# A trunk of two layers on one core: the begin of each SwiGLU layer in a new order, with T4 from B21 - B11 - T3

## What is computed

```python
def rms_norm(x, g):
    xf = x.astype(jnp.float32)
    y = xf * lax.rsqrt(jnp.mean(xf * xf, axis=-1, keepdims=True) + EPS)
    return (y * g.astype(jnp.float32)).astype(x.dtype)

def swiglu_ffn(h, w_gate_up, w_down):
    gu = jnp.einsum('btd,df->btf', h, w_gate_up)
    g, u = gu[..., :D_FF], gu[..., D_FF:]
    return jnp.einsum('btf,fd->btd', jax.nn.silu(g) * u, w_down)

# in trunk, for each layer i:
        h = rms_norm(x, norm_ffn[i])
        x = x + swiglu_ffn(h, ffn_w_gate_up[i], ffn_w_down[i])
```

## Time and profile before

| what | us |
|---|---|
| median of 3 runs | 1784.62 |
| lowest and highest run | 1777.22, 1785.21 |
| the profiled execution | 1782.1 |
| its span, from first to last instruction | 1780.2 |
| PE busy | 1721.0 |
| DVE busy | 1157.1 |
| ACT busy | 747.5 |
| POOL busy | 133.4 |

### The profile page before, as it was taken

The page is one execution under the profiler, slowest core; times in us unless marked ns, Lnnn a source line. Parts: engine busy times, 40 slices in busy tenths (PEclk is TensorE's granted clock), DMA queues, the critical chain, the costliest instruction groups (busy, mean ns, idle before and its releaser), DMA issues.

```text
span 1780.2 us, 21489 instructions
## 1 busy us (share of the span) xinstructions
PE 1721.0 (97%) x7993; PEld 1433.1 (81%) x7993; DVE 1157.1 (65%) x1638; ACT 747.5 (42%) x1145; POOL 133.4 (7%) x108
## 2 busy tenths in 40 slices
PE   7989999999999999999998999889999999999998
PEld 6867888888888888888786888768888888888887
DVE  5586666666656765655778776875665565576744
ACT  5543333333333335444566564443333333343432
POOL 1010000000000003023123212200000000000000
PEclk9799999999999999999999999999999999999999
DMA  5003332332357333334122113032343332393333
GB/s 174 13 12 125 112 119 89 110 104 91 114 197 284 95 101 90 98 101 116 48 54 66 36 42 90 24 125 89 95 126 99 95 118 89 144 341 101 95 97 117
DMA packets 185786, 188.43 MB, mean 106 GB/s; under 512 B 8354, under 2 KB 138452, under 8 KB 185684
## 3 DMA queue, kind: packets, MB, share of 16 engines
q1 hardware_dynamic: 112884, 150.36, 26.0%
q10 hardware_dynamic: 72800, 36.70, 7.2%
HBM read 137.23 MB, written 44.56 MB: 102 GB/s over the span
## 4 chain that ended last, share of the span: by engine, by line
PE 89%; DVE 6%; issue 2%; ACT 2%; DMA 1%; SPq 0%; DVEq 0%; ACTq 0%
PE bank L744 43%; PE bank L769 24%; PE bank L576 16%; PE bank L952 2%; PE bank L589 1%; PE bank L902 1%; PE bank L654 1%; PE bank L875 1%; DVE f_t L1689 1%; DVE ring L1763 1%; PE bank L638 1%; DMA raw<-in_ffn_w_gate_up 0%; DVE raw_max L2185 0%; DMA raw<-act_d 0%; PE bank L791 0%
## 5 line engine op out<-in xcount | busy, mean ns | idle before, releaser
L744 PE MATMUL bank<-h_T,ring 128*128 128x512 f32 x2112 | 505.0, 392 | 16.8 <-DVE ring L1763 10.8
L744 PEld LDWEIGHTS bank<-h_T,ring 128*128 128x128 f32 x2112 | 397.7, 189 | 104.9 <-issue 13.2
L769 PE MATMUL bank<-a,w 128*128 128x512 f32 x1848 | 421.1, 389 | 1.8 <-DVE a L1837 1.8
L769 PEld LDWEIGHTS bank<-a,w 128*128 128x128 f32 x1848 | 346.3, 188 | 74.3 <-issue 2.6
L744 PE MATMUL bank<-h_B,ring 128*128 128x512 f32 x1584 | 381.3, 390 | 6.5 <-DVE ring L1763 6.3
L744 PEld LDWEIGHTS bank<-h_B,ring 128*128 128x128 f32 x1584 | 296.7, 188 | 69.5 <-DVE ring L1763 7.1
L1763 DVE TENSOR_TENSOR ring<-raw,ring 128x512 fp32r<-128x512 f32 (+1 forms) x180 | 146.5, 815 | 48.9 <-ACT ring L1167 48.5
L1167 ACT CAST ring<-raw 128x512 fp32r<-128x512 f32 (+1 forms) x180 | 128.5, 716 | 76.2 <-PE bank L744 54.7
L1833 DVE TENSOR_TENSOR w<-wd_A,w 128x1024 fp32r<-128x1024 f32 x72 | 82.7, 1149 | 101.9 <-ACT w L1238 101.9
L1238 ACT CAST w<-wd_A 128x1024 fp32r<-128x1024 f32 x72 | 70.6, 981 | 178.4 <-PE bank L769 178.4
L576 PE MATMUL bank<-half_hi,aw 128*128 128x512 f32 x320 | 112.6, 405 | 1.9 <-ACT tmp L1443 1.9
(11 more groups left out here) (178 smaller groups left out, 2060.7 us busy)
## 6 DMA issues: line engine op xcount, KB each, us to landing
act_d<-tmp SPq DMA_DIRECT2D x154, 256.0 KB, 3.3
raw<-in_ffn_w_gate_up ACTq DMA_DIRECT2D x70, 512.0 KB, 4.1
raw<-act_d SPq DMA_DIRECT2D x70, 512.0 KB, 3.6
wd_A<-in_ffn_w_down SPq DMA_DIRECT2D x40, 512.0 KB, 8.3
raw<-in_attn_w_qkv SPq DMA_DIRECT2D x24, 512.0 KB, 4.0
raw<-in_ffn_w_gate_up SPq DMA_DIRECT2D x18, 512.0 KB, 4.4
raw<-in_attn_w_o SPq DMA_DIRECT2D x16, 512.0 KB, 4.0
tmp<-tmp SPq DMA_DIRECT2D x80, 64.0 KB, 2.0
```

The lines of the kernel that those rows point to most:

```text
L744: ins = pe.matmul(out[:, :], w, m, start=k in (1, 2, 5) and j == 0 and t == 0, stop=k in (2, 3, 4) and j == 3 and t == 2, skip_group_check ...
L769: ins = pe.matmul(banks[m][:, :], w, h, start=q in (0, 1, 3) and first and t == 0, stop=q in (1, 5, 6) and jj == NBLK - 1 and t == 2, skip ...
```

## The change

Four things are changed, in both layers, and nothing outside the begin of the SwiGLU stage except where the pieces before it are named.

1. **Squares inside the first product.** The two sums of squares on PE stand between the first three (layer 0) or two (layer 1) pieces of product 1 of chunk 0 and its rest; the spread of the scale (`wide`) stands ahead of product 2 of chunk 0 instead of behind it. On ACT the root comes ahead of the copy of product 1, on DVE the reciprocal comes ahead of `swiglu`.
2. **T4 from B21 - B11 - T3.** B21 - B11 is made in place by four new passes (`d_full`): in layer 0 behind the reciprocal, in layer 1 two of them behind a weight split and two behind the reciprocal. `t4_full` subtracts T3 from it and stands beside `t3_lo`. `t2_lo` no longer waits for T4. `h_tp` now counts T3 first and T4 second.
3. **DVE's and ACT's passes.** Chunk 1's first split stands behind the first `b1_full` and `t1_full`; the pair S2, S4 of chunk 0 stands in the middle of T2; `add_c11` of chunks 0 to 2 stands later; `block_sums` of chunk 2 is cut in two parts, of which the first stands ahead of the splits S1 of chunk 2 and A22 of chunk 1; A11 of chunk 3 is split ahead of S3 and A22 of chunk 2. In `pair_sums` the sum for T2 comes ahead of the one for T3. The table `EARLY` follows the new order.
4. **Block products.** Product 3 of chunk 1 comes ahead of product 7 of chunk 0, and product 1 of chunk 3 between products 6 and 3 of chunk 2.

The diff, cut to its core:

```diff
-        EARLY = {0: (1, 3, 5, 5, 2, 2, 4), 1: (6, 10, 11, 12, 13, 7, 14), 2: (8, 15, 16, 16, 17, 9, 18)}
+        EARLY = {0: (1, 3, 9, 9, 2, 2, 4), 1: (5, 10, 11, 12, 13, 6, 15), 2: (7, 14, 16, 16, 18, 8, 19)}
...
             def swiglu(layer):
                 k = 2 * layer + 1
-                gate_up(layer, 0, 1)
+                first = 3 if layer == 0 else 2
+                gate_up(layer, 0, 1, range(first))
                 if layer == 0:
                     sum_square(1, 14, bank[3])
                 else:
                     mean_square(3, 1, bank[3])
                 sum_square(k, 15, bank[3])
+                gate_up(layer, 0, 1, range(first, 4))
+                wide(k, 1, bank[5])
                 gate_up(layer, 0, 2)
-                wide(k, 1, bank[5])
...
                 gate_up(layer, 1, 6)
+                gate_up(layer, 1, 3)
                 gate_up(layer, 0, 7)
-                gate_up(layer, 1, 3)
...
                 for i in range(2, NF):
-                    if i > 2:
+                    if i > 3:
                         gate_up(layer, i, 1)
                     gate_up(layer, i, 5)
                     gate_up(layer, i, 6)
+                    if i == 2:
+                        gate_up(layer, 3, 1)
                     gate_up(layer, i, 3)
...
             def swiglu(layer):
                 k = 2 * layer + 1
+                root(k, 1, bank[3])
                 snap_p1(layer, 0)
-                root(k, 1, bank[3])
                 w_split(layer, 1, G_A11)
+                t1_hi(layer, 0)
                 w_split(layer, 1, G_A12)
...
                 t2_hi(layer, 0)
+                w_split(layer, 0, G_S2, 2)
+                t2_hi(layer, 1)
                 snap_p5(layer, 0)
                 w_split(layer, 1, G_S1)
...
+                w_split(layer, 1, G_S3)
                 silu_1(layer, 0)
-                w_split(layer, 1, G_S3)
-                silu_0(layer, 0)
+                w_split(layer, 2, G_S1)
                 w_split(layer, 1, G_A22)
                 silu_1(layer, 1)
-                w_split(layer, 2, G_S1)
+                w_split(layer, 2, G_S2, 2)
+                silu_0(layer, 0)
                 silu_0(layer, 1)
-                w_split(layer, 2, G_S2, 2)
+                w_split(layer, 3, G_A11)
+                snap_p5(layer, 2)
                 w_split(layer, 2, G_S3)
                 w_split(layer, 2, G_A22)
-                w_split(layer, 3, G_A11)
...
+            def d_full(layer, j):
+
+                dve.wait_ge(h_full, 16 * layer + 4 + j + 1)
+                nc.vector.tensor_tensor(f_t4[:, j, 1, :], f_t4[:, j, 1, :], f_t4[:, j, 0, :], ALU.subtract
+                                        ).then_inc(h_d, 1)
+
             def t4_full(layer, j):
-                dve.wait_ge(h_t, 8 * layer + 4 + j + 1)
-                nc.vector.tensor_tensor(f_t4[:, j, 1, :], f_t4[:, j, 1, :], f_t2[layer][:, j, 1, :], ALU.subtract
+
+                dve.wait_ge(h_d, 4 * layer + j + 1)
+                dve.wait_ge(h_tp, 8 * layer + j + 1)
+                nc.vector.tensor_tensor(f_t4[:, j, 1, :], f_t4[:, j, 1, :], f_t3[:, j, 1, :], ALU.subtract
                                         ).then_inc(h_tp, 1)
...
             w_split(0, 0, G_S1)
             w_split(0, 0, G_A22)
-            w_split(0, 0, G_S2, 2)
+            inverse(1, 1)
+            for j in range(4):
+                d_full(0, j)
 
             def swiglu(layer):
-                inverse(2 * layer + 1, 1)
-                w_split(layer, 1, G_A11)
-                w_split(layer, 1, G_A12)
                 b1_full(layer, 0)
                 t1_full(layer, 0)
+                w_split(layer, 1, G_A11)
                 b1_full(layer, 1)
                 t1_full(layer, 1)
                 t1_lo(layer, 0)
-                add_c11(layer, 0)
+                w_split(layer, 1, G_A12)
                 b1_full(layer, 2)
                 t1_full(layer, 2)
+                t1_lo(layer, 1)
                 w_split(layer, 2, G_A11)
...
                 b1_full(layer, 4)
                 t2_full(layer, 0)
-                t4_full(layer, 0)
                 b1_full(layer, 5)
                 t2_full(layer, 1)
-                t4_full(layer, 1)
                 t2_lo(layer, 0)
-                w_split(layer, 1, G_S1)
+                w_split(layer, 0, G_S2, 2)
                 b1_full(layer, 6)
                 t2_full(layer, 2)
-                t4_full(layer, 2)
                 t2_lo(layer, 1)
+                w_split(layer, 1, G_S1)
...
+                w_split(layer, 1, G_S2)
+                t3_full(layer, 0)
+                t3_full(layer, 1)
+                w_split(layer, 1, G_S4)
+                t3_full(layer, 2)
+                t3_full(layer, 3)
                 for j in range(4):
-                    t3_full(layer, j)
-                w_split(layer, 1, G_S2)
-                for j in range(4):
+                    t4_full(layer, j)
                     t3_lo(layer, j)
+                t4_lo(layer, 0)
+                add_c22(layer, 0)
+                for j in range(1, 4):
+                    t4_lo(layer, j)
+                w_split(layer, 1, G_S3)
+                block_sums(layer, 2, 0)
+                w_split(layer, 2, G_S1)
+                w_split(layer, 1, G_A22)
                 add_c12(layer, 0)
-                w_split(layer, 1, G_S4)
-                for j in range(4):
-                    t4_lo(layer, j)
-                add_c22(layer, 0)
-                w_split(layer, 1, G_S3)
+                add_c22(layer, 1)
+                block_sums(layer, 2, 1)
+                w_split(layer, 2, G_S2, 2)
+                hidden_1(layer, 0)
+                add_c11(layer, 0)
+                hidden_0(layer, 0)
+                pair_sums(layer, 0)
                 add_c12(layer, 1)
...
                 hidden_1(layer, 1)
-                block_sums(layer, 2)
-                w_split(layer, 2, G_S1)
+                add_c11(layer, 1)
                 hidden_0(layer, 1)
-                w_split(layer, 2, G_S2, 2)
+                pair_sums(layer, 1)
+                w_split(layer, 3, G_A11)
                 w_split(layer, 2, G_S3)
-                pair_sums(layer, 1)
                 w_split(layer, 2, G_A22)
-                w_split(layer, 3, G_A11)
+                add_c11(layer, 2)
                 block_sums(layer, 3)
```

More of the change, by code:

```diff
@@ L721, in gate_up @@
                 h = H[layer][moving]
[L722 removed]
+                if 0 not in js:
+                    pass
+                elif k == 1 and i >= 3:
                     pe.wait_ge(s_g0, NF * layer + (1 if i == 4 else i - 1))
```

75 lines of the change are left out of this document (37 added, 38 removed).

## The result

The changed kernel has a median of 1795.97 us in 4 runs (1794.67 to 1799.9), against 1782.17 us in the 4 runs of the kernel before (1777.22 to 1785.21). The ratio is 1.0089, with a 95% interval from 1.0068 to 1.011: slower by 0.9% (the medians alone lie 13.8 us, 0.8%, apart), where the forecast was 1795.0 and slower. The profiled execution took 1794.67 us (span 1792.9), 12.6 more than the one of before (1782.1), where the walk had said 12.0.

The account below looks back on a forecast made before the run. PE, busy 97%, bounds the kernel, with DVE the bound in the splitting stretch. Layer 0's +3.8, layer 1's +4.8 and the clock's 3.4 made 12.0 us on 1782.1: 1794.1, stated as 1795, range 1784 to 1805.

Parts of the forecast that it names:

- Steps 1 to 3: Layer 0's begin: scale ends at 90.8; chunk 1's products 1 and 2 wait 1.3 and 0.8 us, chunk 2's product 1 none.
- part 1's gain: Early squares, root and inverse in layer 0: the scale's spread comes 2.9 us earlier.
- Step 4: DVE's dense stretch: S2/S4 pair adds 1.15 us, POOL's sums 3.2; product 5 of chunk 1 waits 4.5 us.
- the upper bound: POOL's cost to DVE in the dense stretch: 0.6 us above 3.2 if a scaled pass holds POOL off.
- 13.2: Total loss in us instead of 12.0, if DVE and POOL exclude each other for whole instructions, the first to start going first.
- Step 5: PE runs without a wait to 130.6, product 3 of chunk 1 filling T3's split time; 3.7 us ahead of the old order.
- Step 6: Before product 4 of chunk 1: DVE's sums await chunk 2's gate block; PE waits 5.7 us, was 0.79, ending 2.2 behind.
- Step 7: Sixteen more DVE passes make product 1 of chunk 3 wait 3.2 us; product 4 of chunk 2 waits 2.3.
- Clock: Half clock after each layer's first long wait adds 1.7 us, 3.4 in all; after the second it costs nothing.
- A: Rival: price of POOL and of the clock not paid, +2.2 us, or +7 with half unpaid; 1785 to 1790; chance 0.22.
- B: Rival: the start decides and late loads don't; 17 us won, 1766; chance 0.18 for it or a part.
- C: Rival: losses add up further (more half clock, POOL held off, slower chunk 3 load), +16 to +21, 1799 to 1804; chance 0.10.

Follow-up runs that it names:

- squares_back: First half of the change, POOL's two sums held back, S2/S4 pair split behind chunk 1's S1, but squares, spread and root placed as before: 1781.85 us, 1.0002.
- t4_old: First half of the change, POOL's two sums held back, S2/S4 pair split behind chunk 1's S1, but T4 as before (B21 - T2): 1783.02 us, 1.0007.
- pool_late: The changed kernel with POOL's third and fourth sum of chunk 1 held back until T2 is split: 1790.61 us, ratio 1.0051 to the kernel before.
- product3_back: The changed kernel with product 3 of chunk 1 again behind product 7 of chunk 0: 1795.38 us, ratio 1.0091 to the kernel before.
- a22_first: The changed kernel with chunk 1's A22 split and two additions for its product 4 ahead of chunk 2's first block sums: 1793.92 us, 1.0074.
- begin_only: The changed kernel with the old order from chunk 1's split S3 on, so only the change's first half: 1788.15 us, ratio 1.0035 to the kernel before.
- best_join: First half, POOL's sums and S2/S4 pair later, chunk 1's A11 split earlier, needed additions and an ACT copy ahead of load-bound work: 1774.86 us, 0.9970.

## Why the prediction was right

Forecast +12.0 on the profiled run, measured +12.6; forecast slower with the largest chance, and slower it is. By its own steps, each time counted from the begin of product 1 of chunk 0 where the runs' different begin would blur it:

- **Steps 1 to 3** held. The spread that makes the scale ends 7.4 us after the begin, 5.0 without the half clock, as forecast (90.8 - 85.78). Products 1 and 2 of chunk 1 wait 0.94 and 1.29 us, 2.2 together where 2.1 was forecast, and product 1 of chunk 2 has no wait. `squares_back` and `t4_old` show both parts to be worth something, about 1.2 and 1.5 us per stage; the forecast had "most of part 1's gain" spent on the four differences.
- **Step 4** held, and its price was low by half a us. The four passes cost 0.63 + 1.08 + 0.95 + 1.06 = 3.7 us (their rows above less 0.69), against 3.2, and the excess lies wholly in the first pair: 1.7 against 0.5 + 0.6, while the second pair cost 2.0 against 1.0 + 1.1. In the kernel before both of these sums took 1.29 us; now the second took 1.74, and the held-up pass of 93.49, which ended at 94.81, lay between the two. The 0.6 of the upper bound did not come. The order that it supposed did: POOL's third sum, which started 0.16 after a scaled pass of DVE's that reads the scale from SBUF, took 1.70 us, and the first, which started 0.25 after a scaled pass that reads PSUM, took 1.29. But the sum that the forecast read its price from had itself taken 1.75, begun 0.61 after a pass of DVE's with both inputs in SBUF (94.03, 1.21 us), so such a hold was in the price already. "SBUF — State Buffer", "Who interferes with whom", of the Trainium skill says of two such instructions that the first to start goes first; these rows agree, and the 13.2 worked out from it was counted too high at this place. `pool_late` shows the effect of the step: 2.0 us of wait and the half clock behind it, 6.8 us of the time for both layers (0.0038; 7.2 by the stages).
- **Step 5** held in kind: product 3 of chunk 1 does fill the time for T3, all but 0.43 us; `product3_back` shows that without it product 7 waits for 2.66. Its number did not hold: "3.7 ahead" set a walk at full clock against a trace with 1.7 us of half clock. With the 2.2 of clock, the 0.5 of POOL and the 0.43, product 7 of chunk 0 was done 50.6 us after the begin, 48.2 without the half clock there. The old order had done one product less at 131.6, 45.8 after its begin, and would be at 48.5 with it: 0.3 ahead.
- **Step 6** held: 5.10 and 5.14 us before product 4 of chunk 1, ended by the addition, with DVE idle 3.91 us on the load, against 5.7 forecast. The load took half a us less than the 4.4 of idleness that the walk gave. `a22_first` shows that the order makes the wait, and that the order of those passes alone does not make the loss. What the step left out is that the earlier product 3 took 2.7 us of PE's work away from over the load: with it put back the wait falls to 4.29 and 3.42 us, though the time does not.
- **Step 7** is the term that was sized most wrongly: 1.68 and 1.76 us before product 1 of chunk 3, forecast 3.2. The forecast itself said that the second half clock would fall into this wait. It did, 36 matmuls taking 10.25 us where 3 x 2.72 + 0.16 = 8.3 would do, and 3.2 less 1.9 is 1.3. Its time was right for a reason that was partly wrong: from the addition at 143.35 to the split at 155.19 there are fourteen passes, not sixteen, and the rest is a wait of 1.20 us for ACT's cast. The 2.11 and 2.18 before product 4 of chunk 2 are the 2.3 forecast.
- **Clock.** Added 1.7 per layer; measured 2.2 in layer 0 (7.81 against 5.60 for 24 matmuls) and 1.7 in layer 1 (7.32 against the same 5.60).
- **The sum.** 16.8 us in the stages, of which 2.4 is the half clock at the begin of layer 0: 14.4 against the forecast's 12.0. POOL (0.5 in each layer), the clock (0.5) and the waits of 0.43 before the last piece of product 7 are about the difference. The earlier begin of the stage, 4.05, hid it in the span. That the forecast met the time within 1 us is in this part luck; its steps were short by 2 us.

Of the rivals, A (POOL and clock not paid) falls with the rows at 108.68 and 110.24 and with the clock at 0.50. B (the begin decides) fails twice: the late load is in the way, and `begin_only` shows that the begin alone gains nothing in this form, 1.0035. Yet B was right in that something is to be won there: 0.9979 once POOL and the pair stand elsewhere. Of C's additions only POOL held up by DVE came, 0.5 us in each layer and in the first pair; behind the waits before product 1 of chunk 3 and product 4 of chunk 2 the clock stayed full (24 matmuls in 5.69, 36 in 8.51).

What the forecast had not seen is that each half of the change loses by itself, 1.0035 and 1.0045. By step 5 and the word "here" in step 6 it laid all of it on the second; the clock, booked at the end of the sum, hid that the first half had nothing left to lose.

## What to carry to other kernels

- In an engine's in-order queue put what the bound engine needs next ahead of a pass that waits for a load. Moving that one pass is not enough: the passes behind the load move the wait to the next product (5.10 to 0.78 here, and 5.11 in the next place).
- A helper engine's additions can hold up the main vector engine: each of POOL's, 1.3 to 1.7 us long, cost DVE 0.6 to 1.1 us here. Place them by where the vector engine has slack, and hold them back with a wait if the natural moment is in the dense stretch (0.4% here).
- Compare the length of a stage from its own begin, not times from the begin of the run: here 4 us of chance lay in between.

## What was not expected of the hardware

The half clock comes in places that no change touches, and differs from run to run of kernels whose code there is the same. The windows from 46.4 to 60 us, PE alone, changed kernel and then `best_join`:

```profile
46.40:60.00 13.60, 13.60 (x97) 0.87 0.01 2
```

```profile
46.40:60.00 13.60, 13.60 (x73) 0.55 0.01 2
```

In the profiled run of before the same stretch has 0.50 throughout. Over the profiled executions of the twelve kernels of this study product 1 of chunk 0 of layer 0 begins between 80.56 and 89.69 us. Between the two stages, and behind the second, the same executions differ by less than 3 us each, so this is the largest such difference that the traces show. Runs of one kernel spread over 8 us (1777.22 to 1785.21 before) and up to 13 (1791.74 to 1805.02, `product3_back`); whether the same stretch makes that spread is not shown. What decides where it falls was not tried and stays open.

Nor does one length of wait decide it: in the kernel before the half clock followed the wait of 1.81 us in layer 0 (24 matmuls in 7.30) and not the wait of 3.65 in layer 1 (12 in 3.02), nor one of 1.81 there (24 in 5.72); in the changed kernel it followed those of 4.40 and 5.10, and not that of 2.11 (36 in 8.51).
